# The inverse of a chunked gated DeltaNet scan: 16x16 blocks solved on VectorE and GpSimd, three doublings on TensorE

## The reference

```python
a = m + jnp.eye(DN_CHUNK)            # m: strictly lower, (k*beta) k^T * decay within a chunk
u = lax.linalg.triangular_solve(a, v * beta[..., None], lower=True, unit_diagonal=True)
w = lax.linalg.triangular_solve(a, kb * jnp.exp(gc)[..., None], lower=True, unit_diagonal=True)
attn = jnp.where(incl, einsum(q, k) * decay, 0.0)
def step(s, inp):                     # over the chunks
    v_new = ui - wi @ s
    o = qd @ s + ai @ v_new
    s = s * exp(gl) + kd.T @ v_new
```

## Time and profile before

| | us |
|---|---|
| median of 3 runs | 3832.19 |
| lowest and highest run | 3829.12, 3832.26 |
| span of the profiled execution | 3830.5 |
| the stage that is changed, within it | 615.3 (646.2 to 1261.5) |
| TensorE busy in the span | 3625.1 (95%) |
| VectorE, ScalarE, GpSimd busy | 1860.4, 1102.6, 840.9 |

### The profile page before, as it was taken

The page is one execution under the profiler, slowest core; times in us unless marked ns, Lnnn a source line. Parts: engine busy times, 40 slices in busy tenths (PEclk is TensorE's granted clock), DMA queues, the critical chain, the costliest instruction groups (busy, mean ns, idle before and its releaser), DMA issues. The chain is left out here.

```text
span 3830.5 us, 45733 instructions
## 1 busy us (share of the span) xinstructions
PE 3625.1 (95%) x16812; PEld 2319.9 (61%) x16812; DVE 1860.4 (49%) x2861; ACT 1102.6 (29%) x2297; POOL 840.9 (22%) x622
## 2 busy tenths in 40 slices
PE   6999997999999999779999999999978999999998
PEld 2455444888888444434444444445557887887886
DVE  4455554555566654345222322223446666666666
ACT  4266555444444521031111111112211111111113
POOL 1022222443333620020111111113321122112211
PEclk8999999999999999899999999999969999999999
DMA  7122324222221431573111131124434665565566
GB/s 286 43 84 76 99 85 130 67 82 82 82 71 61 160 99 55 176 258 126 55 55 55 55 115 55 45 72 143 146 130 155 209 210 191 205 210 195 202 210 242
DMA packets 286671, 486.28 MB, mean 127 GB/s; under 512 B 18908, under 2 KB 166911, under 8 KB 286377
## 3 DMA queue, kind: packets, MB, share of 16 engines
q1 hardware_dynamic: 263188, 425.33, 32.8%
q0 software_dynamic: 12096, 43.84, 4.4%
q10 hardware_dynamic: 11221, 14.87, 1.1%
HBM read 380.03 MB, written 103.96 MB: 126 GB/s over the span
## 5 line engine op out<-in xcount | busy, mean ns | idle before, releaser
L2660 POOL TENSOR_TENSOR mg<-mg,sg_m 128x512 f32<-128x512 f32 x64 | 98.1, 1533 | 777.7 <-DVE sg_m L2541 777.7
L3547 PE MATMUL bank<-xeT,raw_e 128*128 128x128 f32 x2304 | 267.9, 275 | 0.8 <-ACT xeT L3391 0.8
L3547 PEld LDWEIGHTS bank<-xeT,raw_e 128*128 128x128 f32 x2304 | 263.6, 192 | 8.3 <-issue 8.3
L2447 PE MATMUL bank<-hT,raw_w 128*128 128x512 f32 x576 | 261.8, 597 | 5.2 <-PEq L2251 5.2
L954 POOL TENSOR_SCALAR sg<-tmp 128x512 f32<-128x512 f32 (+1 forms) x76 | 113.4, 1493 | 428.4 <-DVE tmp L1022 368.3
L2447 PEld LDWEIGHTS bank<-hT,raw_w 128*128 128x128 f32 x576 | 110.4, 192 | 144.2 <-issue 144.2
L3547 PE MATMUL bank<-T_e,U 128*128 128x128 f32 x1536 | 176.7, 275 | 0.0
L3547 PEld LDWEIGHTS bank<-T_e,U 128*128 128x128 f32 x1536 | 174.1, 192 | 0.0
L682 PE MATMUL bank<-T_d,S_d 128*128 128x512 f32 x384 | 172.7, 596 | 0.0
L2447 PE MATMUL bank<-zT,S 128*128 128x512 f32 x384 | 172.6, 592 | 0.0
L2510 ACT ACTIVATE sg_m<-sg_m 128x512 f32<-128x512 f32 x72 | 45.4, 631 | 395.0 <-DVE sg_m L2550 395.0
(11 more groups left out here) (527 smaller groups left out, 7260.6 us busy)
## 6 DMA issues: line engine op xcount, KB each, us to landing
raw_e<-in_exp_w_gate SPq DMA_DIRECT2D x16, 3072.0 KB, 16.4
raw_e<-in_exp_w_up SPq DMA_DIRECT2D x16, 3072.0 KB, 13.0
raw_e<-in_exp_w_down SPq DMA_DIRECT2D x16, 3072.0 KB, 10.4
raw_w<-in_w_in SPq DMA_DIRECT2D x24, 1024.0 KB, 5.4
raw_d<-in_w_in SPq DMA_DIRECT2D x16, 1024.0 KB, 5.8
raw_h<-in_w_in SPq DMA_DIRECT2D x12, 1024.0 KB, 5.3
x0T<-in_ada_w SPq DMA_DIRECT2D x44, 256.0 KB, 3.0
kT<-kT_d SPq DMA_DIRECT2D x36, 256.0 KB, 2.9
```

The source lines that it names most:

```text
L2447: mm = pe.matmul(bank[:, :], lhs[:, k, :], rhs[:, k, :], start=first and k == 0, stop=k == 3, skip_group_check=not first)
L2660: pool.tensor_tensor(mg[:, i, :], mg[:, i, :], sg[:, i, :], ALU.add).then_inc(add_ok[i], 1)
L3547: mm = pe.matmul(bank[:, f * P:(f + 1) * P], lhs[:, k, f * P:(f + 1) * P], rhs[:, k, :], start=fresh and k == 0, stop=k == 3, skip_group_c ...
```

## The change

`LEVELS` becomes `[16, 32, 64]`. What stood for the first steps of the inverse (identity, `pair_turn`, `pairs` and the doublings 2, 4 and 8) is gone. In its place the 16x16 diagonal blocks of the inverse are solved by substitution, on small tiles in which a partition holds one block: 8 blocks x 4 heads x 2 steps = 64 partitions of 256 values. VectorE solves the lower triangles (`lower_blocks`), GpSimd the upper ones (`upper_blocks`), two steps at a time, 30 dependent instructions each, of which every one waits for the one before by a semaphore (`link`).

Blocks and matrix change layout through memory. SP stores `Nc` (`store_gram`, to `nc_d`), loads its diagonal blocks in 64-byte runs (`load_blocks`, to `nb`, in space of `gm`), stores the solved blocks in 64-byte runs into an image that is zero elsewhere (`store_blocks`, to `ti_d`) and loads that image as `T` (`load_inverse`). The zeros are written once by four DMAs from a new input `t_zero`, at the start of the projection stage.

Since this takes longer, fronts run four steps ahead (`AHEAD = 4`). `AT` gets ten buffers, four of them in `hTc`, `Nc` four; the front's keys and queries are loaded apart from those of the scan, into `kF` and `qF` in the space of `raw_h`. The weights for `raw_h` and the table for `gm` are therefore loaded in step 14 and no longer at the start of the stage. Doublings are done for all four heads at once, and their parts are put between the products of the scan and of the front. The loop is written out for all 18 steps.

```diff
-LEVELS = [2, 4, 8, 16, 32, 64]
+LEVELS = [16, 32, 64]
+BLK = 16 * P + 16
...
+                    for r in range(4):
+                        sp.dma_start(ti_d[r].rearrange("(p c) -> p c", p=P), A["t_zero"]).then_inc(img_ok, 16)
...
+                    def store_gram(f):
+                        sp.wait_ge(nc_ok, f + 1)
+                        sp.dma_start(nc_d[f].rearrange("(h r) -> h r", r=8 * BLK)[:, 0:P * P].rearrange("h (s c) -> s h c", c=P), Nc[:, f % AHEAD]).then_inc(nc_st[f % 2], 16)
+                    def load_blocks(b):
+                        for w in range(2):
+                            f = 2 * b + w
+                            sp.wait_ge(nc_st[w], 16 * (b + 1))
...
+                            sp.dma_start(nb[b % 2][32 * w:32 * w + 32, :].rearrange("q (i c) -> q i c", c=ROWS), padded(nc_d[f])[:, :, 0:ROWS]).then_inc(nb_in[b % 2], 16)
+                    def load_inverse(m):
+                        sp.wait_ge(tb_st[m % 2], 32 * (m // 2 + 1))
+                        if m >= 2:
+                            sp.wait_ge(F_tr, m - 1)
...
+                    for s in range(STEPS):
+                        if s >= 1:
+                            store_output(s - 1)
+                        if s + 1 < STEPS:
+                            load_keys(s + 1)
+                            load_values(s + 1)
+                        if s % 2 and s + 2 < STEPS:
+                            load_inverse(s + 2)
+                        if s + AHEAD + 1 < STEPS:
+                            load_front(s + AHEAD + 1)
+                        if s + AHEAD < STEPS:
+                            store_gram(s + AHEAD)
+                        if s % 2 and s + AHEAD < STEPS:
+                            load_blocks((s + 3) // 2)
+                        if s % 2 == 0 and s + 2 < STEPS:
+                            store_blocks((s + 2) // 2)
+                            load_inverse(s + 2)
...
+                    def lower_blocks(b, half):
+                        x, t = nb[b % 2], Tb[:, b % 2, 0, :]
...
+                            link(dve.tensor_copy(t, unit))
+                            link(dve.tensor_scalar(grid(t)[:, 1:ROWS, 0], x[:, 1:ROWS], -1.0, None, ALU.mult))
+                        for k in (range(1, HALF) if half == 0 else range(HALF, ROWS - 1)):
+                            area = [64, ROWS - 1 - k, k + 1]
+                            work = prod_f[:, 0:(ROWS - 1 - k) * (k + 1)].rearrange("q (i c) -> q i c", c=k + 1)
+                            link(dve.tensor_tensor(work, x[:, k * ROWS + k + 1:(k + 1) * ROWS].unsqueeze(2).to_broadcast(area), grid(t)[:, k:k + 1, 0:k + 1].to_broadcast(area), ALU.mult))
+                            link(dve.tensor_tensor(grid(t)[:, k + 1:ROWS, 0:k + 1], grid(t)[:, k + 1:ROWS, 0:k + 1], work, ALU.subtract))
```

More of the change, by code:

```diff
@@ L69, in shape_tables @@
     tri = np.stack([ui, li, su, sl], 1).astype(np.float32)
-    pair = (r == (c ^ 1)).astype(np.float32)
     lv = [(r // (2 * b) == c // (2 * b)) & (r // b != c // b) for b in LEVELS]
@@ new lines, in merge_outer, with inverse_turned @@
+                    def merge_outer(m, l):
+                        pe.wait_ge(P_ok, level(m, l))
+                        pe.wait_ge(TT_ok, level(m, l))
+                        mm4(2, TTm, E1).then_inc(U_mm, 1)
+                    def inverse_turned(m):
+                        pe.wait_ge(up_ok, level(m, NL - 1))
+                        for d in range(2):
+                            for h in heads:
+                                last = pe.transpose(b4(d)[:, h, :], T[:, m % 2, d, h, :], eye[:, :])
+                        last.then_inc(F_tr, 1)
@@ new lines, in _ @@
+                    decays(0)
+                    decays(1)
+                    for d in range(2):
+                        masked(0, d)
+                    decays(2)
+                    for d in range(2):
+                        masked(1, d)
+                    for d in range(2):
+                        masked(2, d)
+                    upper_blocks(0, 0)
+                    upper_blocks(0, 1)
+                    decays(3)
+                    for d in range(2):
+                        masked(3, d)
@@ L1466, in _ @@
                 @block.vector
                 def _(dve):
-                    dve.sem_inc(o_ok, 2)
-                    for q in range(4):
-                        dve.sem_inc(o_st[q], 16)
                     for d in range(2):
@@ L1550, in _, with gram @@
-                    all_steps(dve, step)
+                    def gram(f, d):
+                        dve.wait_ge(kk_mm, nth(f, d))
+                        dve.wait_ge(Em_ok, nth(f, d))
+                        if d and f >= 1:
+                            dve.wait_ge(nc_ok, f)
+                        dst = N2[:, :, :] if d else Nc[:, f % AHEAD]
+                        for h in heads:
+                            last = dve.scalar_tensor_tensor(dst[:, h, :], attn(f, d)[:, h, :], column(beta, f, d, h), b4(front_bank(f, 1 + d))[:, h, :], ALU.mult, ALU.mult)
+                        last.then_inc(n_ok, 1)
@@ new lines, in front @@
+                    def front(f):
+                        for d in range(2):
+                            gram(f, d)
+                        gram_sum(f)
+                        for d in range(2):
+                            attention(f, d)
+                    for f in range(AHEAD - 1):
+                        front(f)
+                    lower_blocks(0, 0)
+                    lower_blocks(0, 1)
+                    front(AHEAD - 1)
+                    for l in range(NL):
+                        crossed(0, l)
+                        joined(0, l)
@@ new lines, in _ @@
+                    lower_blocks(1, 0)
+                    for s in range(STEPS):
+                        f, m = s + AHEAD, s + 1
+                        ahead, merging = f < STEPS, m < STEPS
+                        rest(s, 0)
+                        rest(s, 1)
+                        if s % 2 == 0 and s + 2 < STEPS:
+                            lower_blocks((s + 2) // 2, 1)
+                        if merging:
+                            crossed(m, 0)
+                        if ahead:
+                            gram(f, 0)
+                        state_added(s, 0)
+                        if merging:
+                            joined(m, 0)
+                        state_added(s, 1)
+                        if ahead:
+                            gram(f, 1)
+                        if merging:
+                            crossed(m, 1)
+                        if ahead:
+                            gram_sum(f)
+                        if merging:
+                            joined(m, 1)
+                        output_added(s, 0)
+                        if ahead:
+                            attention(f, 0)
+                        output_added(s, 1)
+                        if merging:
+                            crossed(m, 2)
+                        if ahead:
+                            attention(f, 1)
+                        if merging:
+                            joined(m, 2)
+                        if s % 2 and ahead:
+                            lower_blocks((s + 3) // 2, 0)
```

664 lines of the change are left out of this document (360 added, 304 removed).

## The result

| | time, us | profiled span, us | ratio to before, 95% interval |
|---|---|---|---|
| before | 3830.65 (3826.63 to 3832.26) | 3830.5 | 1 |
| changed | 3706.74 (3699.36 to 3708.23) | 3706.4 | 0.9673 [0.9659, 0.9687] |
| changed, run again later | 3703.47 (3700.55 to 3709.67) | 3707.9 | 0.9664 [0.9651, 0.9678] |

The kernel before is here the median of four runs; the three in its own table give 3832.19. The forecast was 3720, its main case 3700 to 3750, its whole range 3668 to 3798. The profiled spans differ by 124.1 us, where the sum had 113. The page after, against the earlier trace rows: span, then busy time, share and records by engine.

A forecast was written before the change was run, and what follows sets the result against it. TensorE (95% busy) bounds the kernel before; afterwards the order of small chained operations binds. The stage's terms sum to 497 us against 610.6, 113 less: 3830.5 - 113 + 1.7 = 3719, taken as 3720, range 3668 to 3798.

The forecast's parts named there:

- main case: Whole kernel: small chained operations delay even steps to 30.2 us, odd ones take 22.5; 3720 us, chance 0.47.
- opening: Stage start until the first `mm4(kT, S)`: four fronts, 30 links in one run, three doublings; 56 us instead of 33.1.
- six pairs: Steps 2 to 13, each pair an even step of 30.2 us and an odd one of 22.5; 6 x 52.7 = 316.
- X: Time into the even step when the first half of the links ends and `rest` can start; 6.9 us.
- The shared access: Even step: VectorE links with two SBUF inputs get in one per long GpSimd operation, six alternating with six.
- no hindrance: Rival: VectorE and GpSimd do not hinder each other at this size; even step 24 us, total 3671; chance 0.2.
- From X to `crossed`: Even step: `rest`, six links alternating with long GpSimd operations, eight beside GpSimd's links at 0.42 us; 11.5 us.
- From `crossed` to the end of the step: Even step, to TensorE's last product: mask, outer product, `joined`, two more doublings with other products between, no slack; 11.8 us.
- formula in c: c is one GpSimd link's time beside VectorE's links, taken as 0.42 us; one pair of steps costs 42.6 + 24c.
- dear links: Rival: a GpSimd link costs 0.75 us, a pair 60.6, the opening 66, step 14 34; total 3790; chance 0.23.
- slower: Rival: GpSimd links cost still more; the stage's gain is gone at 0.95 us, total 3866 at 1.1; chance 0.08.
- late-trip rival: Rival: the round trip through memory costs three more us per pair on SP's queue; 3741, no separate chance.

The follow-up runs named there:

- split version: Changed kernel with first half behind `rest`, VectorE's products and block rows in PSUM, lower and upper inverses stored and loaded apart; 3655.18 us (0.9545).
- PSUM run: Changed kernel with VectorE's block rows and products in PSUM bank 2, so no product or subtraction has two SBUF inputs; 3666.76 us (0.958).
- run with the second load: Changed kernel with each load of the inverse `T` issued twice, the second after the first has landed; 3726.0 us (0.9731).
- run with the first half moved: Changed kernel with the first half of the block solving moved from the odd step's end to behind `rest` in the even step, in SBUF; 3721.41 us (0.9723).

## Where the prediction was right and where it was wrong

| | forecast, us | measured |
|---|---|---|
| opening | 56 | 63.1 |
| step 0, step 1 | 28, 22.5 | 28.3, 22.1 |
| six pairs | 316 | 307.1 |
| step 14 | 26 | 24.7 |
| steps 15 and 16 | 38 | 36.5 |
| last step | 10.6 | 10.7 |
| sum | 497 | 492.5 |
| behind the stage | 0 | -5.2, spread |

- **TensorE's own time.** 196 records in an odd step at the pace of the earlier trace rows, 22.08 us with no wait at all; the 0.6 us charged for waits was not needed.
- **The links.** GpSimd's were put at 0.42 us from two sizes of its long operations and one gap: 0.35 to 0.36 on average in the even step shown, 0.21 to 0.34 of it work. VectorE's alone: 0.245 forecast, 0.21 to 0.25 measured. X: 6.9 forecast, 5.6 to 6.05 measured.
- **The shared access.** Six long links beside six long operations were forecast from one scaling and `Nc`, and six came. That was the term with a rival, and the runs settle it: one input in PSUM takes the links from 1.1 to 0.21 us, and ten long operations make ten long links. The "no hindrance" rival (even 24) is refuted.
- **From X to `crossed`.** 11.5 forecast, 10.2 measured: 1.2 for `rest`, 6.65 for the six, 2.3 for the eight, which go at 0.29 and not 0.42: the last three, of 15 to 28 elements, take only 0.17 to 0.18.
- **From `crossed` to the end of the step.** 11.8 forecast; 13.1 measured. In the split version it is 11.79 at clock 1.00, so the path was right, and the step that failed is that the sum never asked what TensorE's clock does after a gap of 3.3 us. It is the same omission as in the opening: the three doublings were put at 10 us and took 18.0, at 0.50 to 0.56, where the PSUM run needed 11.9 at 1.00; so 6.1 us are the clock and 1.9 a sum that was too short. Both were in the profile before as a possibility: clock 0.87 over the old opening. Such a wait does not always have that price: in step 0 of the run with the second load TensorE waited 3.27 us for `crossed`, the clock stayed at 1.00 and the step took 26.6 us, not 28.3.
- **The errors cancel.** Per pair +1.3 for the clock against -0.9 and -1.3 for links and -0.4 for the odd step; over the stage +7.1 for the opening against -11.6 for the rest. The sum is off by 4.5 us, the terms by more; that it comes so close is partly luck.
- **The formula in c did not tell two things apart.** It had 24 us of a pair hang on each us of c, sixteen of them through X and eight through VectorE's second half. If GpSimd's work doubles by the number of its operations, that is wrong: 13 us in all where it has 83, because `rest` waits only for VectorE's own first half and GpSimd's later R takes the place of another wait. So GpSimd's work on the blocks has room for twice its amount; the odd steps began to pay there (22.27 once). If each operation became longer, VectorE's links would be expected to go with them, as they do beside its long ones, and X with them. The rivals "dear links" (3790 at c = 0.75) and "slower" (from 0.95), with 31 in 100 and the range's upper end, meant that case; it did not come about, and their prices are neither confirmed nor refuted.
- **Memory.** The landing at 2.5 us with 4.3 free was 1.7 to 3.0 with 4.2 free. The late-trip rival did not come about. Its price of a us per us of delay was paid in the run with the second load, from 4.2 us on.

The Trainium skill, SBUF — State Buffer, section "SBUF: two separate sides", was weighed in the prediction for the exclusive lock against VectorE operations with two SBUF inputs. By the PSUM run that holds for these small links too: long ones of 0.96 to 1.20 us with two inputs in SBUF, 0.21 with one in PSUM. The copy and the scaling of the run with the first half moved, with one input in SBUF each, waited too, which the prediction had not reckoned with.

## What to carry to other kernels

A small VectorE operation with both inputs in SBUF took here about as long as the operation that GpSimd ran beside it; so count GpSimd's operations in the window, not VectorE's, and put one input in a PSUM bank that is idle then (40 us here; 44 with the first half behind `rest`, a reordering that cost 15 without it; 51 with the split loads as well). Taking work from GpSimd can make it worse, if that work was short and kept the long ones away. And a sum for a kernel that TensorE bounds needs a term for the clock after each new gap: 3.3 us of waiting cost 1.3 more in the even step shown and nothing in one step 0, and behind a wait of 2.95 us the three doublings of the opening cost 6.1 more.

## What the runs showed of the hardware beyond that

- GpSimd's chained two-input operations on 64 x 15 to 64 elements take 0.21 to 0.34 us in the even step shown, one every 0.28 to 0.42 us; VectorE's, with an input in PSUM or GpSimd idle, 0.16 to 0.23, one every 0.20 to 0.26. With both chains running and all inputs in SBUF, VectorE's takes GpSimd's pace, 0.34 to 0.38, on 48 to 64 elements.
- The stretch behind the stage, with the same code in all kernels, spans 10.6 us over the fourteen profiles. Differences of a few us between two profiles there say nothing of a change.
